# Up products on the unscaled residual, scaled in PSUM, with every second residual addition on GpSimd

## The chip, the cores and the metric

The kernel runs on one core of a Trainium2 chip. Five engines work side by side, each with its own in-order instruction queue: TensorE (PE, matmuls into PSUM), VectorE (DVE), ScalarE (ACT), GpSimd (POOL, which doesn't reach PSUM) and SyncE (SP, which here issues DMAs). They wait for each other on semaphores. The metric is the device time of one execution in microseconds, and lower is better.

## The reference, cut to what matters

The program computes a first block of two layers (attention and a recurrent mixer side by side, then a feed-forward part and an embedding gate) and a second block of two layers, on 512 tokens of width 1024, all in float32. The change touches one place of the first block's layers:

```python
x = x + rmsnorm(mixed @ w_out, norm_mix_post)
h = rmsnorm(x, norm_ffn_pre)                      # y * rsqrt(mean(y*y) + eps) * gain
u = causal_dwconv(h @ w_up, conv_w, conv_b)       # three taps along the tokens, per channel
ua, ub = _split(u, (FFN_DIM, FFN_DIM))            # 2816 = 22 tiles of 128 each
x = x + rmsnorm((jax.nn.gelu(ua) * ub) @ w_down, norm_ffn_post)
```

The root-mean-square factor of a token multiplies its whole row of `h`, so it can be taken out of the product `h @ w_up`: scaling each token's column of the product gives the same numbers.

## The kernel before, in words

Activations lie transposed: 128 partitions of channels, then tiles of 128 channels (KD = 8 for the width), then 512 tokens. The residual is `xT` [128, 8, 512]. A matmul makes a tile of 128 output channels by 512 tokens, one PSUM bank; there are 8 banks, of which bank 6 holds the spread factor of a norm (`rstd`) or the running sums of the modulation, and bank 7 the column sums of a norm.

For accuracy each float32 operand is split into a high part (rounded to the fast matmul format) and a low part (the rest). A product is three matmuls per k tile (`split_matmuls`, L232): high x high weight, low x high weight, high x low weight, so 24 for a tile over the width. Weights come as a stream of units of 512 KB in the order of use. For each unit SP loads it into one of two raw buffers (L309), ACT copies it to its high part `Whi` (L284), GpSimd subtracts to get the low part `Wlo` (`low_parts`, L299), into one of three slots. `HighParts.upto` lets ACT make a high part only once the unit three before is used up; ACT, GpSimd and SP do this at fixed places of their queues. SP loads a unit once the low part of the unit two before is done, and issues the modulation weights (`ada_load`) between the units of the feed-forward part.

At the change the order is this. The out projection leaves `yT`. Its norm "n2" is made: squares on ACT, sums over channels on PE (`column_sums`, 16 records of one column each, L178), root on ACT (L146), reciprocal on DVE (L217), spread of the four token columns to a [128, 512] factor on PE (`norm_spread_pe`, L205). Then `residual_dve` (L1854, L1857) does eight times a multiplication T (`yT` by gain and factor into `t2`) and an addition A (`xT` + `t2`). ACT squares each new tile (L133), PE sums it, and after the eighth comes the root, the reciprocal and the spread of norm "n3". Only then `split_dve` and `split_act` make the scaled tile (L392), its high part `hh` on ACT (L367) and its low part `hl` on DVE (L386), tile by tile, and PE starts the first two up products together (`split_pair`: for each k tile three matmuls for the one and three for the other, as soon as `hl` is there).

The feed-forward part follows a list, `FFN1`: up products (i, 0) and (i, 1) for i = 0 to 21, into banks 2(i % 2) and 2(i % 2) + 1, with the down products of eight hidden tiles put in after i = 9 and 17 and at the end. For each up product ACT makes `acc` = bank x tap 2 + bias (L1992), DVE adds taps 1 and 0 (L2043, L2046); ACT's gelu (L1974) of (i, 0) goes back into its bank, DVE multiplies with (i, 1) (L2023), ACT makes the high part `gh` (L1980) and DVE the low part `gl` (`g_low`, L2027). PE may start (i, 0) once `g_low(i - 2)` is done. During the first 48 entries of the list DVE also does two modulation steps each (`mods_dve`, L336, L340). PE's sums for these steps are L349.

Of the kernel before, what the change touches and what calls it, by code (L numbers as in the profile page):

```python
# [18 lines left out]
F32 = mybir.dt.float32  # L19
# [8 lines left out]
P = 128  # L28
# [1774 lines left out]
    mixed_low_dve(dve, s, b, KD - 2, KD)  # L1803


def split_product(pe, ps, w, b):

    for k in range(KD):
        last = split_matmuls(pe, ps, columns_of(w, 1, at=k * P), tiles_of(b["hh"][:, k:k + 1], b["hl"][:, k:k + 1]), 1,
                             start=k == 0, stop=k == KD - 1)  # L1810
    return last


def split_pair(pe, ready, banks, units, b, done):

    for k in range(KD):
        pe.wait_ge(ready, k + 1)
        for ps, w in zip(banks, units):
            last = split_matmuls(pe, ps, columns_of(w, 1, at=k * P), tiles_of(b["hh"][:, k:k + 1], b["hl"][:, k:k + 1]), 1,
                                 start=k == 0, stop=k == KD - 1)  # L1820
            if k == KD - 1:
                last.then_inc(done, 1)


def project_pe(pe, s, b, ring, done, copied, ready, name, later=None):
# [15 lines left out]
def copy_act(act, b, mm, copied, dst, high, first, after, n=8, func=ACT.Copy):  # L1841
    for m in range(n):
        high.around(act, first + m)
        act.wait_ge(mm, m + 1)
        act.activation(dst[:, m], b["ps"][:, m % 4], func).then_inc(copied, 1)
        after(m)


def residual_dve(dve, s, b, step, y, gain):
# [75 lines left out]
def ffn_pe(pe, s, b, ring):  # L1925
    for at, key in enumerate(FFN1[0]):
        if 0 <= at - SUM_LAG < MODS and (at - SUM_LAG) % ADA_N == ADA_N - 1:
            mods_pe(pe, s, b, (at - SUM_LAG) // ADA_N)
        if key[0] == "up":
            i, j = key[1:]  # L1930
            if i == 0:
                if j == 0:
                    pair = [ring.take(pe) for _ in range(2)]
                    split_pair(pe, s["h2_lo"], [b["ps"][:, x] for x in range(2)], pair, b, s["up_p"])
                continue
            w = ring.take(pe)
            if i >= 2:
                pe.wait_ge(*((s["up_v"], UP_V(i - 2, "b2")) if j else (s["g_lo"], i - 1)))
            split_product(pe, b["ps"][:, 2 * (i % 2) + j], w, b).then_inc(s["up_p"], 1)
        elif key[1] < PARTS1 - 1:  # L1940
            down_pe(pe, s, b, ring, key[1], key[2], FT)
        elif key[2] >= OPEN:
            down_pe(pe, s, b, ring, key[1], key[2], FT)
            if key[2] == KD - 1:
                summed_squares_pe(pe, s, b, "n4")
        elif key[2] == 0:
            pe.wait_ge(s["mods_v"], 1)
            last_down_pe(pe, s, b, ring, FT)
# [22 lines left out]
def ffn_act(act, s, b, high, first):  # L1971
    def gelu(i):
        act.wait_ge(s["up_v"], UP_V(i, "a2"))
        act.activation(b["ps"][:, 2 * (i % 2)], b["acc"][:, 2 * (i % 2)], ACT.Gelu_apprx_tanh).then_inc(s["up_ge"], 1)  # L1974

    def g_high(i):
        act.wait_ge(s["up_g"], i + 1)
        if i >= GRING:
            act.wait_ge(s["dn_p"], KD * ((i - GRING) // PART + 1))
        act.activation(b["gh"][:, i % GRING], b["ps"][:, 2 * (i % 2)], ACT.Copy).then_inc(s["g_hi"], 1)  # L1980

    for key in FFN1[0]:
        high.around(act, first + FFN1[1][key])
        if key[0] == "up":
            i, j = key[1:]
            slot = 2 * (i % 2) + j
            if j == 1:
                gelu(i)
            act.wait_ge(s["up_p"], 2 * i + j + 1)
            if i >= 2 and j == 1:  # L1990
                act.wait_ge(s["up_g"], i - 1)
            act.activation(b["acc"][:, slot], b["ps"][:, slot], ACT.Identity, scale=b["p"]("cw2", j * FT + i),  # L1992
                           bias=b["p"]("cb", j * FT + i)).then_inc(s["up_a"], 1)
            if j == 0 and i:
                g_high(i - 1)
            if j == 1 and i == FT - 1:
                high.upto(act, first + FFN1[1][("down", PARTS1 - 1, OPEN - 1)] + 1)
                table_act(act, b, "n4", ACT.Sqrt)
                g_high(i)
        elif key[1] == PARTS1 - 1:  # L2000
            for m in (key[2] - 1,) if key[2] < KD - 1 else range(key[2] - 1, KD):
                if m >= 0:
                    act.wait_ge(s["dn_v"], KD * (PARTS1 - 1) + m + 1)
                    summed_square_act(act, s, b, "n4", m, b["yT"][:, m])
# [13 lines left out]
def ffn_dve(dve, s, b):  # L2018
    def product(i):
        dve.wait_ge(s["up_ge"], i + 1)  # L2020
        dve.wait_ge(s["up_v"], UP_V(i, "b2"))
        bank = b["ps"][:, 2 * (i % 2)]
        dve.tensor_tensor(bank, bank, b["acc"][:, 2 * (i % 2) + 1], MUL).then_inc(s["up_g"], 1)  # L2023

    def g_low(i):
        dve.wait_ge(s["g_hi"], i + 1)
        dve.tensor_tensor(b["gl"][:, i % GRING], b["ps"][:, 2 * (i % 2)], b["gh"][:, i % GRING].bitcast(F32), SUB).then_inc(s["g_lo"], 1)  # L2027

    for at, key in enumerate(FFN1[0]):
        if at == MODS + SUM_LAG + 1:  # L2030
            dve.wait_ge(s["m_p"], MODS)
            dve.tensor_copy(b["mods"][:, b["layer"]], b["ps"][:, b["norm_bank"], 0:MODS]).then_inc(s["mods_v"], 1)
        if key[0] == "down":
            down_dve(dve, s, b, key[1], key[2])
            if key[1] == PARTS1 - 1:
                square_sum_dve(dve, s, b, "n4", key[2] - 2)
            if at < MODS:
                mods_dve(dve, s, b, at)
            continue
        i, j = key[1:]  # L2040
        slot = 2 * (i % 2) + j
        dve.wait_ge(s["up_a"], UP_A(i, ("ca", "cb")[j]))
        dve.scalar_tensor_tensor(out=b["acc"][:, slot, 1:TOK], in0=b["ps"][:, slot, 0:TOK - 1], scalar=b["p"]("cw1", j * FT + i),  # L2043
                                 in1=b["acc"][:, slot, 1:TOK], op0=MUL, op1=ADD).then_inc(s["up_v"], 1)
        dve.wait_ge(s["up_v"], UP_V(i, "ab"[j] + "1"))
        dve.scalar_tensor_tensor(out=b["acc"][:, slot, 2:TOK], in0=b["ps"][:, slot, 0:TOK - 2], scalar=b["p"]("cw0", j * FT + i),  # L2046
                                 in1=b["acc"][:, slot, 2:TOK], op0=MUL, op1=ADD).then_inc(s["up_v"], 1)
        if j == 0 and i:
            g_low(i - 1)
        if j == 1:  # L2050
            product(i)
            if i == FT - 1:
                g_low(i)
        if at < MODS:
            mods_dve(dve, s, b, at)

# [39 lines left out]
def first_block(nc, b, stream, stream_after, ple, ada, positions):  # L2098
# [1 line left out]
        [f"ada_in{i}" for i in range(ADA)] + ["md_v", "m_p", "mods_v"] + [f"w_in{i}" for i in range(RAW)] + ["w_hi", "w_lo", "ple_in", "zeroed", "x_out", "x_back"] + \  # L2100
        norms("n2", "n3", "n4", "n5", "nx") + [n + x for n in ("h1", "h2") for x in SPLIT_SEMS] + \
        ["res1", "res2", "res3"] + RWKV_SEMS + ATT_SEMS + ["gate_p", "gate_a", "gate_v", "mx_hi", "mx_lo", "wo_p", "wo_z"] + \
        ["up_p", "up_a", "up_v", "up_ge", "up_g", "g_hi", "g_lo", "dn_p", "dn_v", "p_hi", "p_lo", "e_p", "e_z",
         "h3_hi", "h3_lo", "pg_p", "pg_z", "pg_v"]
    with ExitStack() as ctx:
        s, every = semaphores(ctx, nc, names)
# [10 lines left out]
        with ExitStack() as c:  # L2117
# [17 lines left out]
            with ExitStack() as c2:  # L2135
                sb(c2, "yT", KD, TOK)
                with ExitStack() as c3:
                    for name in ("gh", "gl"):
                        sb(c3, name, GRING, TOK, dt=F32R)
                    for name, *shape in (("acc", 4, TOK), ("ada", ADA, UNIT), ("macc", 2, ADA_W)):  # L2140
                        sb(c3, name, *shape)
                with ExitStack() as c3:
                    sb(c3, "pT", 2, TOK)
# [7 lines left out]
        for layer in range(LAYERS):  # L2151
            enter_layer(b, layer, stream[layer], stream[layer + 1] if layer + 1 < LAYERS else stream_after[0])
            with nc.Block() as block:
# [32 lines left out]
                def _(pool):  # L2186
# [7 lines left out]
                    attention_masks(pool, s, b)  # L2194
                    low_parts(pool, s, b, AT_ATT + 8, AT_GATE + 3)
                    attention_pool(pool, s, b)
                    low_parts(pool, s, b, AT_GATE + 3, AT_E + 2)
                    pool.wait_ge(s["p_hi"], 1)
                    pool.tensor_tensor(b["pl"][:], b["pT"][:], b["ph"][:].bitcast(F32), SUB).then_inc(s["p_lo"], 1)
                    low_parts(pool, s, b, AT_PG, AT_PG + 1)  # L2200
# [8 lines left out]
                def _(pe):  # L2209
# [8 lines left out]
                    pe.wait_ge(s["gate_a"], 16)  # L2218
                    project_pe(pe, s, b, ring, s["wo_p"], s["wo_z"], s["mx_lo"], "n2")
                    norm_spread_pe(pe, s, b, "n2")  # L2220
                    norm_pe(pe, s, b, "n3", KD)
                    ffn_pe(pe, s, b, ring)
                    norm_spread_pe(pe, s, b, "n4")
                    for m in range(KD):
# [15 lines left out]
                def _(act):  # L2240
# [19 lines left out]
                    def square_y(m):  # L2260
                        act.wait_ge(s["wo_z"], m + 1)
                        summed_square_act(act, s, b, "n2", m, b["yT"][:, m])
                    copy_act(act, b, s["wo_p"], s["wo_z"], b["yT"], high, AT_WO, square_y)
                    norm_root_act(act, s, b, "n2", 1, D)
                    norm_act(act, s, b, "n3", lambda i: b["xT"][:, i], KD, D, lambda i: (s["res1"], 2 * i + 2))
                    split_act(act, s, "h2", b, b["hh"], KD)
                    ffn_act(act, s, b, high, AT_FFN)
                    norm_root_act(act, s, b, "n4", 1, D)
                    act.wait_ge(s["ple_in"], 16)
# [21 lines left out]
                def _(dve):  # L2291
# [8 lines left out]
                        square_sum_dve(dve, s, b, "n2", i)  # L2300
                    norm_dve(dve, s, "n2", b)
                    dve.wait_ge(s["x_back"], 16)
                    residual_dve(dve, s, b, s["res1"], b["yT"], lambda i: b["p"]("mix_post", i))
                    norm_dve(dve, s, "n3", b)
                    split_dve(dve, s, "h2", b, scaled(dve, b, b["xT"], lambda i: b["p"]("ffn_pre", i)), b["hh"], b["hl"], KD)
                    dve.wait_ge(s["tab_out"], 32)
                    ffn_dve(dve, s, b)
                    norm_dve(dve, s, "n4", b)
# [862 lines left out]
```

## Time and profile before

| | us |
|---|---|
| median of 3 runs | 3939.98 (3936.72 to 3941.65) |
| span of the profiled execution (first to last instruction) | 3931.4 |
| own time of the profiled execution | not listed apart from its span |
| PE busy | 3743.9 (95%) |
| DVE busy | 1848.1 (47%) |
| ACT busy | 1581.7 (40%) |
| POOL busy | 1779.5 (45%) |
| DMA | 379.88 MB, mean 97 GB/s |
| mean granted TensorE clock | 0.979 |

Busy time counts the instructions on the engine itself, not its waits. A timeline row gives the start in us from the span's start, the duration, the engine, the line of the kernel, what it writes and reads, and in brackets how long the engine idled before it and what ended that. The granted clock is 1.00 at 2.4 GHz and 0.50 at 1.2 GHz.

### The profile page before, as it was taken

The page shows a single profiled execution, that of the slowest core. Times are in us where ns is not written, and L with a number is a line of the kernel's source. Part 1 is how long each engine was busy: PE and PEld are TensorE (multiplying, and loading weights), DVE is VectorE, ACT ScalarE, POOL GpSimd, SP SyncE. Part 2 cuts the span into 40 slices and gives each one's busy share as a digit, 9 for nine tenths or more (in the row PEclk, how much of TensorE's full clock was granted, in tenths as well). Part 3 has the DMA queues.
Part 4 walks back from the last instruction along what each step waited for, and adds up shares of the span by engine and source line. Part 5 has one row for each costly group of instructions (what it writes and reads, how often), then busy time and mean ns, then how long its engine had stood idle before and what let it go on. Part 6 is the DMA issues. An engine that isn't in the chain of part 4 may idle for free. (4 is left out here: it accounts for less than half of the span.)

```text
span 3931.4 us, 72626 instructions
## 1 busy us (share of the span) xinstructions
PE 3743.9 (95%) x30890; PEld 3040.7 (77%) x30904; DVE 1848.1 (47%) x2868; ACT 1581.7 (40%) x2643; POOL 1779.5 (45%) x1132
## 2 busy tenths in 40 slices
PE   7999989999998999998999999899999999999998
PEld 6777758878887777776887887677878877787887
DVE  7777652155635877754226553543231133423112
ACT  5555352343334555535234333454332234433222
POOL 5555444434445555544443444463444435344443
PEclk9999999989998999999998999899999999999999
DMA  4111203335532211122334553212222221222322
GB/s 142 52 56 56 88 28 135 99 134 193 183 107 76 92 51 56 56 99 72 99 105 143 189 182 104 69 65 76 97 86 97 97 85 66 70 96 87 97 97 86
DMA packets 108753, 379.88 MB, mean 97 GB/s; under 512 B 12560, under 2 KB 12944, under 8 KB 107792
## 3 DMA queue, kind: packets, MB, share of 16 engines
q1 hardware_dynamic: 102816, 365.66, 27.8%
q10 hardware_dynamic: 5616, 9.58, 0.7%
q8 instruction: 246, 4.03, 0.4%
q14 instruction: 75, 0.61, 0.1%
HBM read 359.46 MB, written 15.73 MB: 95 GB/s over the span
## 5 line engine op out<-in xcount | busy, mean ns | idle before, releaser
L299 POOL TENSOR_TENSOR Wlo<-raw,Whi 128x1024 fp32r<-128x1024 f32 (+1 forms) x744 | 1385.8, 1876 | 1671.6 <-ACT Whi L284 1671.4
L232 PE MATMUL ps<-hh,Whi 128*128 128x512 f32 x2864 | 1150.9, 402 | 22.1 <-DVE hl L383 10.1
L232 PE MATMUL ps<-hl,Whi 128*128 128x512 f32 x2864 | 1125.3, 393 | 0.0
L232 PE MATMUL ps<-hh,Wlo 128*128 128x512 f32 x2864 | 1124.4, 393 | 0.1
L284 ACT ACTIVATE Whi<-raw 128x1024 fp32r<-128x1024 f32 x552 | 578.7, 1054 | 689.3 <-PE ps L232 617.8
L232 PEld LDWEIGHTS ps<-hh,Whi 128*128 128x128 f32 x2864 | 543.3, 190 | 147.8 <-issue 15.7
L232 PEld LDWEIGHTS ps<-hh,Wlo 128*128 128x128 f32 x2864 | 543.0, 190 | 116.2 <-issue 0.5
L232 PEld LDWEIGHTS ps<-hl,Whi 128*128 128x128 f32 x2864 | 543.8, 190 | 108.1 <-issue 1.9
L232 PE MATMUL ps<-gh,Whi 128*128 128x512 f32 x864 | 337.9, 391 | 3.8 <-POOL Wlo L299 3.8
L232 PE MATMUL ps<-gh,Wlo 128*128 128x512 f32 x864 | 336.5, 390 | 0.0
L232 PE MATMUL ps<-gl,Whi 128*128 128x512 f32 x864 | 336.5, 389 | 0.0
L1146 POOL TENSOR_TENSOR TM<-TD,const 128x256 f32<-128x256 f32 x192 | 157.4, 843 | 152.3 <-PE ps L719 75.7
L1799 DVE TENSOR_TENSOR sg<-sg,ps 128x512 f32<-128x512 f32 x64 | 44.0, 688 | 366.9 <-PE ps L232 366.6
L232 PEld LDWEIGHTS ps<-gh,Whi 128*128 128x128 f32 x864 | 162.2, 188 | 39.0 <-POOL Wlo L299 5.5
L232 PEld LDWEIGHTS ps<-gh,Wlo 128*128 128x128 f32 x864 | 162.2, 188 | 33.8
L232 PEld LDWEIGHTS ps<-gl,Whi 128*128 128x128 f32 x864 | 162.3, 188 | 33.2
L2736 DVE SCALAR_TENSOR_TENSOR xT<-ps,mod,xT 128x512 f32<-128x512 f32 x64 | 48.1, 752 | 281.7 <-PE ps L232 281.7
L1992 ACT ACTIVATE acc<-ps,par 128x512 f32<-128x512 f32 x88 | 68.6, 780 | 273.5 <-PE ps L232 273.5
L2726 DVE TENSOR_TENSOR gt<-gt 128x512 f32<-128x512 f32 x64 | 47.9, 749 | 256.8 <-ACT gt L2614 256.8
L2043 DVE SCALAR_TENSOR_TENSOR acc<-ps,par,acc 128x511 f32<-128x511 f32 x88 | 66.0, 750 | 197.7 <-ACT acc L1992 197.7
L1782 ACT ACTIVATE sg<-ps 128x512 f32<-128x512 f32 x64 | 38.3, 599 | 239.2 <-PE ps L232 239.2
L719 PEld LDWEIGHTS ps<-X,TM 64*64 64x64 f32 x2560 | 81.8, 135 | 55.7 <-DVE y L1216 32.1
(365 smaller groups left out, 5652.8 us busy)
## 6 DMA issues: line engine op xcount, KB each, us to landing
raw<-in_stream SPq DMA_DIRECT2D x554, 512.0 KB, 3.3
ada<-in_ada SPq DMA_DIRECT2D x96, 512.0 KB, 4.3
park_x<-xT SPq DMA_DIRECT2D x2, 2048.0 KB, 7.3
park_yh<-yh ACTq DMA_DIRECT2D x16, 256.0 KB, 2.1
park_yl<-yl ACTq DMA_DIRECT2D x16, 256.0 KB, 2.5
xT<-park_x SPq DMA_DIRECT2D x2, 2048.0 KB, 8.3
yrh<-park_yh SPq DMA_DIRECT2D x16, 256.0 KB, 5.1
yrl<-park_yl SPq DMA_DIRECT2D x16, 256.0 KB, 4.9
```

The lines of the kernel that those rows point to most:

```text
L232: last = pe.matmul(ps, left[a](k), right[c](k), start=start and k == 0 and i == 0, stop=stop and k == n - 1 and i == 2)
L284: act.activation(self.b["Whi"][:, weight_slot(self.b, u)], self.b["raw"][:, raw_slot(self.b, u)], ACT.Copy).then_inc(self.s["w_hi"], 1)
L299: last = pool.tensor_tensor(b["Wlo"][:, slot, part], b["raw"][:, raw_slot(b, u), part], b["Whi"][:, slot, part].bitcast(F32), SUB)
L719: return pe.matmul(b["ps"][half(u), bank, block(c)], left[:, block(c)], right[:, block(c)], start=True, stop=True)
L1146: pool.tensor_tensor(blocks(b["TM"][:, h, l % 2]), blocks(b["TD"][:, h]), lvl[:, l].broadcast_to([P, BLK, CB]), MUL) .then_inc(s["inv_g"], 1)
L1782: act.activation(b["sg"][:, i], b["ps"][:, i], ACT.Sigmoid).then_inc(s["gate_a"], 1)
L1799: dve.tensor_tensor(b["sg"][:, i], b["sg"][:, i], b["ps"][:, 4 + i], MUL).then_inc(s["gate_v"], 1)
L1992: act.activation(b["acc"][:, slot], b["ps"][:, slot], ACT.Identity, scale=b["p"]("cw2", j * FT + i), bias=b["p"]("cb", j * FT + i)).then_i ...
L2043: dve.scalar_tensor_tensor(out=b["acc"][:, slot, 1:TOK], in0=b["ps"][:, slot, 0:TOK - 1], scalar=b["p"]("cw1", j * FT + i), in1=b["acc"][: ...
L2726: dve.tensor_tensor(b["gt"][:, i % 4], b["gt"][:, i % 4], b["gt"][:, i % 4], MUL).then_inc(s["f1_v"], 1)
L2736: dve.scalar_tensor_tensor(out=b["xT"][:, m], in0=b["ps"][:, 4 + i % 3], scalar=b["mod"][:, 40 + m:41 + m], in1=b["xT"][:, m], op0=MUL, op ...
```

## The change: what it does

`hh` and `hl` are now made from `xT` times the gain alone, without the factor of norm "n3": ACT's high part is a copy with a scale, DVE's low part is one multiply-and-subtract (`raw_low`). They can follow each addition at once. `shared_residual_dve` does all eight T, the additions of tiles 0, 2, 4 and 6, and the low part of the tile before; `shared_residual_pool` does the additions of tiles 1, 3, 5 and 7 on GpSimd. ACT copies and squares each tile. `summed_pair` on PE does the first two up products tile by tile and puts the column sum of norm "n3" behind each tile's six matmuls. The spread of "n3" moves into product (1, 0), behind its first k tile; ACT stores the spread factor as `r3`. Every one of the 44 up products is then multiplied with `r3` in its bank by DVE (semaphore `up_n`) before ACT reads it. On DVE, `g_low` of the tile before and the modulation steps move ahead of the two tap additions; on ACT, `g_high` moves ahead of `acc`. ACT makes the high part of the third up unit ahead of the root of "n2", and GpSimd its low part ahead of its additions.

```diff
-def split_product(pe, ps, w, b):
+def split_product(pe, ps, w, b, amid=None):
     for k in range(KD):
+        if amid and k == amid[0]:
+            amid[1]()
...
+def summed_pair(pe, s, b, name, banks, units, done):
+    for k in range(KD):
+        pe.wait_ge(s["h2_lo"], k + 1)
+        for ps, w in zip(banks, units):
+            last = split_matmuls(pe, ps, columns_of(w, 1, at=k * P), tiles_of(b["hh"][:, k:k + 1], b["hl"][:, k:k + 1]), 1,
+                                 start=k == 0, stop=k == KD - 1)
+            if k == KD - 1:
+                last.then_inc(done, 1)
+        norm_sum_pe(pe, s, b, name, k, KD)
...
+def raw_low(dve, s, b, i, gain):
+    dve.wait_ge(s["h2_hi"], i + 1)
+    dve.scalar_tensor_tensor(out=b["hl"][:, i], in0=b["xT"][:, i], scalar=gain, in1=b["hh"][:, i].bitcast(F32), op0=MUL, op1=SUB) \
+        .then_inc(s["h2_lo"], 1)
+
+def added(s, i):
+    return s["add_g" if i % 2 else "add_v"], i // 2 + 1
+
+def shared_residual_dve(dve, s, b, gain, pre):
+    for i in range(KD):
+        if i >= 2:
+            dve.wait_ge(*added(s, i - 2))
+        dve.scalar_tensor_tensor(out=b["t2"][:, i % 2], in0=b["yT"][:, i], scalar=gain(i), in1=b["rstd"][:], op0=MUL, op1=MUL) \
+            .then_inc(s["res1"], 1)
+        if i % 2 == 0:
+            dve.wait_ge(s["res1"], i + 1)
+            dve.tensor_tensor(b["xT"][:, i], b["xT"][:, i], b["t2"][:, i % 2], ADD).then_inc(s["add_v"], 1)
+        for k in (i - 1,) if i < KD - 1 else (i - 1, i):
+            if k >= 0:
+                raw_low(dve, s, b, k, pre(k))
+
+def shared_residual_pool(pool, s, b):
+    for i in range(1, KD, 2):
+        pool.wait_ge(s["res1"], i + 1)
+        pool.tensor_tensor(b["xT"][:, i], b["xT"][:, i], b["t2"][:, i % 2], ADD).then_inc(s["add_g"], 1)
...
@@ ffn_pe @@
-                    split_pair(pe, s["h2_lo"], [b["ps"][:, x] for x in range(2)], pair, b, s["up_p"])
+                    summed_pair(pe, s, b, "n3", [b["ps"][:, x] for x in range(2)], pair, s["up_p"])
...
-            split_product(pe, b["ps"][:, 2 * (i % 2) + j], w, b).then_inc(s["up_p"], 1)
+            split_product(pe, b["ps"][:, 2 * (i % 2) + j], w, b, amid=(1, lambda: norm_spread_pe(pe, s, b, "n3")) if i == 1 and j == 0 else None) \
+                .then_inc(s["up_p"], 1)
@@ ffn_act @@
             if j == 1:
                 gelu(i)
-            act.wait_ge(s["up_p"], 2 * i + j + 1)
+            elif i:
+                g_high(i - 1)
+            act.wait_ge(s["up_n"], 2 * i + j + 1)
...
-            if j == 0 and i:
-                g_high(i - 1)
@@ ffn_dve @@
+        if i == 0 and j == 0:
+            dve.wait_ge(s["r3_a"], 1)
+        dve.wait_ge(s["up_p"], 2 * i + j + 1)
+        dve.tensor_tensor(b["ps"][:, slot], b["ps"][:, slot], b["r3"][:], MUL).then_inc(s["up_n"], 1)
+        if j == 0 and i:
+            g_low(i - 1)
+        if at < MODS:
+            mods_dve(dve, s, b, at)
         dve.wait_ge(s["up_a"], UP_A(i, ("ca", "cb")[j]))
...
-        if j == 0 and i:
-            g_low(i - 1)
...
-        if at < MODS:
-            mods_dve(dve, s, b, at)
@@ first_block: GpSimd, PE, ACT, DVE @@
-                    low_parts(pool, s, b, AT_GATE + 3, AT_E + 2)
+                    low_parts(pool, s, b, AT_GATE + 3, AT_FFN + SLOTS)
+                    pool.wait_ge(s["x_back"], 16)
+                    shared_residual_pool(pool, s, b)
+                    low_parts(pool, s, b, AT_FFN + SLOTS, AT_E + 2)
...
-                    norm_pe(pe, s, b, "n3", KD)
...
+                    high.upto(act, AT_FFN + SLOTS)
                     norm_root_act(act, s, b, "n2", 1, D)
-                    norm_act(act, s, b, "n3", lambda i: b["xT"][:, i], KD, D, lambda i: (s["res1"], 2 * i + 2))
-                    split_act(act, s, "h2", b, b["hh"], KD)
+                    for i in range(KD):
+                        act.wait_ge(*added(s, i))
+                        act.activation(b["hh"][:, i], b["xT"][:, i], ACT.Copy, scale=b["p"]("ffn_pre", i)).then_inc(s["h2_hi"], 1)
+                        norm_square_act(act, s, b, "n3", i, b["xT"][:, i])
+                    norm_root_act(act, s, b, "n3", KD, D)
+                    act.wait_ge(s["n3_sp"], 1)
+                    act.activation(b["r3"][:], b["rstd"][:], ACT.Copy).then_inc(s["r3_a"], 1)
...
-                    residual_dve(dve, s, b, s["res1"], b["yT"], lambda i: b["p"]("mix_post", i))
-                    norm_dve(dve, s, "n3", b)
-                    split_dve(dve, s, "h2", b, scaled(dve, b, b["xT"], lambda i: b["p"]("ffn_pre", i)), b["hh"], b["hl"], KD)
+                    shared_residual_dve(dve, s, b, lambda i: b["p"]("mix_post", i), lambda i: b["p"]("ffn_pre", i))
+                    dve.wait_ge(s["n3_rt"], 1)
+                    dve.reciprocal(b["rt"][:], b["rt"][:]).then_inc(s["n3_rs"], 1)
```

## Rows read from the trace of the kernel before

**Rows 1.** Page, part 1: busy us (share of span) xinstructions, by engine.

```profile
PE 3743.9 (95%) x30890; PEld 3040.7 (77%) x30904; DVE 1848.1 (47%) x2868; ACT 1581.7 (40%) x2643; POOL 1779.5 (45%) x1132
```

**Rows 2.** Windows: length, busy us by engine, PEclk, DMA share, GB/s.

```profile
802.10:822.40 20.30, 11.66 (x186) 10.19 (x185) 13.48 (x22) 8.05 (x14) 0.00 (x0) 0.59 0.18 52
835.10:1160.00 324.90, 324.90 (x1585) 266.89 (x1584) 170.63 (x241) 115.51 (x146) 141.67 (x59) 1.00 0.49 172
2059.10:2079.80 20.70, 12.09 (x185) 10.44 (x185) 13.43 (x22) 8.05 (x14) 0.00 (x0) 0.56 0.17 53
```

**Rows 3.** Timeline, DVE: start, us, engine, line, operation, tiles [idle before].

```profile
804.47 0.18 DVE L217 RECIPROCAL rt<-rt 128x4 f32<-128x4 f32 x1 [11.18 <-ACT rt L146]
805.39 0.75 DVE L1854 SCALAR_TENSOR_TENSOR t<-yT,par,ps 128x512 f32<-128x512 f32 x1 [0.74 <-PE ps L205]
806.18 0.69 DVE L1857 TENSOR_TENSOR xT<-xT,t 128x512 f32<-128x512 f32 x1
...
2062.85 0.75 DVE L1854 SCALAR_TENSOR_TENSOR t<-yT,par,ps 128x512 f32<-128x512 f32 x1 [1.21 <-PE ps L205]
```

**Rows 4.** Timeline of ACT, same columns.

```profile
804.18 0.26 ACT L146 ACTIVATE rt<-ps,const 128x4 f32<-128x4 f32 x1 [0.73 <-PE ps L178]
806.90 0.63 ACT L133 ACTIVATE sq<-xT 128x512 f32<-128x512 f32 x1 [2.46 <-DVE xT L1857]
...
830.51 1.04 ACT L284 ACTIVATE Whi<-raw 128x1024 fp32r<-128x1024 f32 x1
...
840.76 0.78 ACT L1992 ACTIVATE acc<-ps,par 128x512 f32<-128x512 f32 x1 [0.84 <-PE ps L232]
...
846.20 0.78 ACT L1992 ACTIVATE acc<-ps,par 128x512 f32<-128x512 f32 x1 [1.34 <-PE ps L232]
...
2104.63 0.78 ACT L1992 ACTIVATE acc<-ps,par 128x512 f32<-128x512 f32 x1 [1.33 <-PE ps L232]
```

**Rows 5.** Timeline of PE at the hole of the first layer.

```profile
804.71 0.65 PE L205 MATMUL ps<-const,rt 128*128 128x128 f32 x4 [0.58 <-DVE rt L217]
807.59 1.02 PE L178 MATMUL ps<-const,sq 128*64 128x1 f32 x16 [2.23 <-ACT sq L133]
...
822.38 0.77 PE L232 MATMUL ps<-hh,Whi 128*128 128x512 f32 x1 [2.39 <-DVE hl L386]
...
824.22 0.63 PE L232 MATMUL ps<-hl,Whi 128*128 128x512 f32 x1
824.65 0.63 PE L232 MATMUL ps<-hh,Wlo 128*128 128x512 f32 x1
```

**Rows 6.** Timeline of PE around one column sum between two products, second block.

```profile
3263.14 0.39 PE L232 MATMUL ps<-hh,Wlo 128*128 128x512 f32 x1
3263.46 0.63 PE L178 MATMUL ps<-const,sq 128*64 128x1 f32 x16
3264.02 0.50 PE L232 MATMUL ps<-hh,Whi 128*128 128x512 f32 x1
```

**Rows 7.** Timelines, GpSimd and DVE; line L2205 (ns min/median/max).

```profile
831.64 2.39 POOL L299 TENSOR_TENSOR Wlo<-raw,Whi 128x1024 fp32r<-128x1024 f32 x1 [30.22 <-ACT Whi L284]
...
1199.31 2.50 DVE L1857 TENSOR_TENSOR xT<-xT,t 128x512 f32<-128x512 f32 x1
...
L2205 POOL TENSOR_TENSOR hl<-xT,hh x16: 1280/1567/1752, 1205.5 to 2478.1; 128x512 fp32r<-128x512 f32 x16
```

**Rows 8.** Windows of PE: busy us (instructions), then PEclk, the granted clock.

```profile
806.00:818.00 12.00, 7.87 (x126) 0.50 0.03 12
822.40:826.10 3.70, 3.70 (x9) 0.50 0.02 4
2079.80:2085.60 5.80, 5.78 (x14) 0.50 0.01 1
```

**Rows 9.** DVE in the products: timeline row of L2023, and a window's busy time.

```profile
840.65 0.70 DVE L2023 TENSOR_TENSOR ps<-ps,acc 128x512 f32<-128x512 f32 x1
...
860.00:900.00 40.00, 25.40 (x37) 1.00 0.53 188
```

More of the change, by code:

```diff
@@ L2102, in first_block @@
         ["res1", "res2", "res3"] + RWKV_SEMS + ATT_SEMS + ["gate_p", "gate_a", "gate_v", "mx_hi", "mx_lo", "wo_p", "wo_z"] + \
-        ["up_p", "up_a", "up_v", "up_ge", "up_g", "g_hi", "g_lo", "dn_p", "dn_v", "p_hi", "p_lo", "e_p", "e_z",
+        ["add_v", "add_g", "up_p", "up_n", "r3_a", "up_a", "up_v", "up_ge", "up_g", "g_hi", "g_lo", "dn_p", "dn_v", "p_hi", "p_lo", "e_p", "e_z",
          "h3_hi", "h3_lo", "pg_p", "pg_z", "pg_v"]
@@ L2139, in first_block @@
                         sb(c3, name, GRING, TOK, dt=F32R)
-                    for name, *shape in (("acc", 4, TOK), ("ada", ADA, UNIT), ("macc", 2, ADA_W)):
+                    for name, *shape in (("r3", TOK), ("acc", 4, TOK), ("ada", ADA, UNIT), ("macc", 2, ADA_W)):
                         sb(c3, name, *shape)
```

## The prediction

> **What bounds the kernel now.** I read the page first: TensorE (PE) is busy 95% of the span, DVE 47%, ACT 40% [rows 1]. So time can be won only where PE waits. The windows of the stages show where that is around the change. In the up and down products (835.1 to 1160.0) PE is busy 324.90 of 324.90 us at the granted clock 1.00, which is 2.4 GHz. Just ahead of them, 802.1 to 822.4, it is busy 11.66 of 20.30 us, at 0.59 on average; the second layer has the same hole, 12.09 of 20.70 us [rows 2]. The change works in these two holes and in the 44 up products behind each. The timelines of DVE, ACT and PE then give the chain in the hole: residual multiplication (T, L1854) and addition (A, L1857) on DVE, eight times; squares on ACT; column sums on PE; root; spread; only then the scaled and split tiles and, at 822.38, the first up matmul [rows 3 to 5]. I measure each layer from the first T (805.39 and 2062.85) to ACT's reading of the fourth up product, called (1,1), at 846.20 and 2104.63 [rows 3, 4]: 40.81 and 41.78 us. From there on PE is the bound, and what is won up to it is won at the end.
>
> The profiled execution has a span of 3931.4 us; the runs' median is 3939.98, 8.6 us more, which lies around the span. I work out differences in the span and add them to the median.
>
> **The change, part by part.** *Ahead of the chain.* ACT now makes the high part of the third up unit (1.04 us) before the root, where it idled 0.73 us [rows 4]: +0.3 us. GpSimd's low part of that unit (2.39 us [rows 7]) moves forward too and runs from about 804.5 to 806.9; SP then issues its next weight load and modulation load some 25 us earlier, into a DMA that is busy 0.18 here [rows 2], at no cost. The first A, at 806.5, reads two SBUF operands. Such an A took 2.50 us beside a low part, against 0.69 alone [rows 7, 3]. It would wait here until 806.9: +0.45 (bounds 0 and 1.8).
>
> *First matmul.* T to A 0.79, the wait 0.45, A 0.69, ACT's scaled copy 0.63 (the square's row [rows 4]), the new low part L 0.75 (as T), hand-overs 0.35: 3.65 us after T. With the 0.3 PE starts at 809.35, where it was 822.38. If GpSimd's first addition gets the port ahead of L, add up to 1.3.
>
> *GpSimd's additions.* Their nearest row is its 128x512 subtraction, 1.28 to 1.75 us [rows 7]. For two tiles DVE has two T, one A and two L, about 3.4 us; when the two-operand ones wait for GpSimd, 3.9 to 4.4. The last L is then ready between 823.5 and 825.3, while PE, by the next part, reaches the last tile at 823.5 at the earliest: PE's pace covers them. Without that cover (PE at full clock throughout, 1.75 for each addition) they would cost 1.8 us a layer. The Trainium skill (GPSIMD Engine Reference, Engine selection) advises elementwise work on VectorE, because two-input operations take about twice as long on GpSimd. By that rule alone four additions, each some 0.7 us longer, would add 2.8 us a layer; the rows agree on the ratio, but the chain they would lengthen is not PE's.
>
> *The pair with the sums in it.* Each of eight k tiles is six matmuls and one column sum of 16 records. At 2.4 GHz a product of 24 matmuls takes 5.44 us (846.20 less 840.76 [rows 4]), 0.227 each, and a sum between products takes 0.88 - 0.23 = 0.65 [rows 6]: 1.36 + 0.65 = 2.01 per tile, 16.1 in all. At 1.2 GHz they start 0.43 apart and a sum takes 1.02 [rows 5]; with 0.1 for the switch 2.56 + 1.12 = 3.7, 29.6 in all. So it matters how long PE stays at 1.2 GHz after 809.35. If that is x us, the pair lasts 16.1 + 0.457x (0.457 = 1 - 2.01/3.7).
>
> *What x is.* No row shows this mixture; both of its parts have rows. Sums alone (busy 7.87 of 12 us) leave the clock at 0.50, and matmuls back to back have it at 0.50 for 3.7 us in one layer and 5.8 in the other before it rises [rows 8]. The bounds are therefore 4.8 (the mean of these) and 29.6 (the whole pair). Weighted by the mixture, 70% matmuls, it would be 12.2; the middle of the bounds is 17.2. The mixture is nearer to back-to-back matmuls, but not the same, so I take 14.5, between the two.
>
> *Behind the pair.* Product (1,0) is 5.44 us, and the spread in its middle 0.65 [rows 5]: PE would be done with it 6.1 us after the pair. The root chain up to the spread hides under three matmuls (0.26 and 0.18 [rows 4, 3] against 0.68). What is late next is the unit of (1,1): its high part stands on ACT behind the first acc, which waits for the new multiplication, which waits for the stored spread. Root 0.26, reciprocal 0.18, spread 0.65, copy 0.63 (as the square), multiplication 0.70 (a row with PSUM in and out [rows 9]), acc 0.78, high part 1.04, low part 2.39, hand-overs 0.5: 7.1. So PE waits 1.0 us there, and (1,1) is read 7.1 + 5.44 + 0.05 = 12.6 after the pair.
>
> *The sum.* 809.35 + 16.1 + 0.457x + 12.6 = 838.05 + 0.457x against 846.20: -8.15 + 0.457x. The second layer was 0.97 us longer before and starts alike: -9.1 + 0.457x. With x = 14.5: -1.5 and -2.5, together **-4.0 us: 3936**.
>
> *In the products.* The 88 added multiplications (0.70 each, 62 us of DVE) I cost at nothing: PE hides them. DVE is busy 25.40 of 40 us early in the products [rows 9], 3.45 per 5.44 us of a product; 4.15 with the new one. The longest new chain, product to multiplication to acc to two convolution steps to product to low part, has a whole further product's time on PE in front of its consumer. Queued behind the waiting multiplication on DVE are only g_low and the modulation steps. With that cover gone the price is rival 3's.
>
> **The rivals.**
> 1. *The clock comes back as promptly as behind dense products*: x = 4.8 in both layers, -6.0 and -6.9, **3927**. For it: matmuls are 70% of the mixture, and once the clock is up, products with sums between them keep it there [rows 6]. Against: in neither layer did a rise come with sums running.
> 2. *The clock stays at 1.2 GHz through the pair* (the slower side). Then x = 29.6, and product (1,0) begins at half speed as well: 2.4 us lost there, of which the 1.0 us wait covers part, so 1.4. -8.15 + 13.5 + 1.4 = +6.8, and +5.8: **3952.6**. It decides from x = 18 on, where the gain is gone. For it: the sums of the kernel before hold 0.50 although PE is busy two thirds of the time [rows 8], and the change puts one behind every sixth matmul. Against: full-width matmuls still take most of each tile. The Trainium skill (TensorE: Matmul & The Clock Gate, "A second HAM failure mode") tells of a kernel whose short idle times between groups of matmuls kept dropping its clock; by that the time would be this rival's, and no row here shows such a mixture at 1.2 GHz.
> 3. *DVE becomes the bound of the products*: all 88 multiplications come to stand on PE's path, +62 us, **4002**. It decides when DVE's work per product passes 5.44 us; 4.15 speaks against it, and a mixture of waits at the start of the products is all that speaks for it.
>
> That the change doesn't do what it says (first matmul not earlier, because A or L waits) would need more than 12 us of port waits; the rows give 3 at most.
>
> **How the numbers follow.** Forecast (x between about 8 and 22, so 3930 to 3943) 0.43; rival 1 0.30; rival 2 0.21; rival 3 0.04; the rest 0.02. A measurement of this kernel can tell about 0.2%, 7.9 us, from no change. Faster by more: rival 1 and the forecast's fast end, 0.35. Slower by more: rivals 2 and 3, 0.25. Within: 0.40. The range runs from a little below rival 1 to rival 2, 3926 to 3952; DVE-bound and worse is left out.
>
> **What would show it.** In the profile after: the first up matmul some 13 us earlier than before after the first T; a low part of 2.4 us under the first A; PE without idle through the pair; the granted clock 0.50 there for x us, which by itself puts the result between rivals 1 and 2; a wait of PE of about 1 us for the low part ahead of (1,1); no idle of PE from there to the down products. Wrong would be PE waiting for L inside the pair (then the additions or the port set the pace), PE waiting for g_low in the products, or a time outside 3926 to 3952.

## The result and the profile after

The changed kernel takes 3944.45 us (median of 20 runs, 3934.87 to 3952.25) against 3939.1 us for the kernel before (3932.5 to 3944.16, 20 runs): ratio 1.0015, interval 1.0008 to 1.0022. It is slower by 5.3 us, inside the range and inside the 0.2%, but not in the direction of the forecast, and the interval leaves out 1. The spread of its runs has grown as well, from 11.7 to 17.4 us. The profiled execution has a span of 3942.2 us.

PE, busy for 3743.9 us before [rows 1], is now busy for longer, although no product was added (page, part 1):

```profile
PE 3759.3 (95%) x30904; PEld 3045.7 (77%) x30904; DVE 1894.1 (48%) x2932; ACT 1589.8 (40%) x2645; POOL 1790.9 (45%) x1140
```

The windows at the two holes of [rows 2] say why. Columns: stretch and length, busy us of PE, PEld, DVE, ACT and POOL with instructions, granted clock, DMA share, GB/s. Of each layer the first row runs up to the first up matmul.

```profile
802.10:813.79 11.69, 6.03 (x70) 4.75 (x68) 4.63 (x6) 4.76 (x9) 6.00 (x3) 0.83 0.50 169
813.79:816.60 2.81, 2.81 (x6) 1.78 (x6) 2.77 (x5) 1.31 (x3) 0.18 (x1) 0.50 0.24 96
816.60:832.24 15.64, 15.64 (x171) 11.71 (x170) 10.29 (x12) 6.99 (x11) 4.10 (x3) 1.00 0.01 2
832.24:839.35 7.11, 6.19 (x32) 4.82 (x29) 5.05 (x9) 5.08 (x7) 2.38 (x1) 1.00 0.00 0
839.35:1160.00 320.65, 320.65 (x1564) 263.30 (x1565) 193.03 (x278) 114.12 (x142) 139.34 (x58) 1.00 0.48 171
2059.10:2069.97 10.87, 5.21 (x66) 4.07 (x64) 4.62 (x6) 4.24 (x8) 5.79 (x3) 0.81 0.52 171
2069.97:2100.00 30.03, 30.03 (x171) 21.63 (x172) 11.26 (x16) 8.18 (x14) 4.25 (x3) 0.50 0.02 10
2100.00:2110.90 10.90, 9.98 (x53) 7.98 (x52) 8.40 (x13) 6.74 (x10) 4.79 (x2) 1.00 0.23 85
```

The same instructions run in both layers. In the first the clock is back at 2.4 GHz 2.8 us after the first up matmul; in the second PE works through nearly the whole pair, 30.0 us without idle, at 1.2 GHz. The timeline of PE in the second layer (start, us, engine, line, operation, tiles, idle before) shows two tiles there: 3.78 us from 2069.97 to 2073.75 and 3.80 from there to 2077.55. Six matmuls 0.43 apart make 2.6 of that; the column sum and the switches to and from it make the other 1.2. The rows before to compare are [rows 5].

```profile
2069.97 0.77 PE L232 MATMUL ps<-hh,Whi 128*128 128x512 f32 x1 [4.66 <-DVE hl L1866]
...
2072.24 0.63 PE L232 MATMUL ps<-hh,Wlo 128*128 128x512 f32 x1
2072.80 1.02 PE L178 MATMUL ps<-const,sq 128*64 128x1 f32 x16
2073.75 0.79 PE L232 MATMUL ps<-hh,Whi 128*128 128x512 f32 x1
...
2077.55 0.79 PE L232 MATMUL ps<-hh,Whi 128*128 128x512 f32 x1
```

As the measure of a layer I take the time from its first T to its first down matmul, since PE has no idle from the fourth product to there. The rows of the down matmul (before, then after) and of the second layer's first T after:

```profile
936.21 0.39 PE L232 MATMUL ps<-gh,Whi 128*128 128x512 f32 x1
2194.64 0.39 PE L232 MATMUL ps<-gh,Whi 128*128 128x512 f32 x1
...
935.18 0.39 PE L232 MATMUL ps<-gh,Whi 128*128 128x512 f32 x1
2203.16 0.39 PE L232 MATMUL ps<-gh,Whi 128*128 128x512 f32 x1
...
2065.35 0.75 DVE L1879 SCALAR_TENSOR_TENSOR t<-yT,par,ps 128x512 f32<-128x512 f32 x1 [0.74 <-PE ps L205]
```

With the first T of [rows 3] and the one at 809.16 below this makes 130.82 and 131.79 us before, 126.01 and 137.81 after: 4.8 gained, 6.0 lost.

The remaining 9.6 of the 10.8 us between the two profiled spans lie outside these stretches. Of them 3.8 are there before the first T (805.39 before, 809.16 after), where the change moves only one weight unit's high part (+0.3 in the prediction), and 3.5 lie between the first layer's down matmul and the second layer's first T, which took 1126.6 us before and 1130.2 after. Both vary from profile to profile: in two further profiles of the changed kernel the second took 1130.1 and 1126.8.

The timelines of DVE and GpSimd at the start of the first layer, to compare with [rows 3] and [rows 7]:

```profile
809.16 0.75 DVE L1879 SCALAR_TENSOR_TENSOR t<-yT,par,ps 128x512 f32<-128x512 f32 x1 [0.74 <-PE ps L205]
809.95 1.08 DVE L1883 TENSOR_TENSOR xT<-xT,t 128x512 f32<-128x512 f32 x1
810.95 0.73 DVE L1879 SCALAR_TENSOR_TENSOR t<-yT,par,ps 128x512 f32<-128x512 f32 x1
811.82 1.82 DVE L1866 SCALAR_TENSOR_TENSOR hl<-xT,par,hh 128x512 fp32r<-128x512 f32 x1
```

```profile
808.13 2.34 POOL L299 TENSOR_TENSOR Wlo<-raw,Whi 128x1024 fp32r<-128x1024 f32 x1 [3.03 <-ACT Whi L284]
811.83 1.26 POOL L1893 TENSOR_TENSOR xT<-xT,t 128x512 f32<-128x512 f32 x1 [1.35 <-DVE t L1879]
```

The first addition took 1.08 us beside the low part of the weights, and the first low part 1.82 beside GpSimd's first addition. PE's two waits in the first layer are the one ahead of the pair and the one foreseen ahead of product (1,1):

```profile
813.79 0.76 PE L232 MATMUL ps<-hh,Whi 128*128 128x512 f32 x1 [4.66 <-DVE hl L1866]
...
839.35 0.50 PE L232 MATMUL ps<-hh,Whi 128*128 128x512 f32 x1 [0.92 <-POOL Wlo L299]
```

### The profile page after: what moved, and what is told of

Its sections match the earlier page's. It is cut to its first block and busy times, and to the rows that moved or that the text cites. A ratio compares the mean times of both kernels' runs of the same rounds, so it can differ in the third digit from the quotient of the medians.

```text
span 3942.2 us, 72688 instructions
## 1 busy us (share of the span) xinstructions
PE 3759.3 (95%) x30904; PEld 3045.7 (77%) x30904; DVE 1894.1 (48%) x2932; ACT 1589.8 (40%) x2645; POOL 1790.9 (45%) x1140
## 3 DMA queue, kind: packets, MB, share of 16 engines
q8 instruction: 246, 4.03, 0.4%
## 5 line engine op out<-in xcount | busy, mean ns | idle before, releaser
L2674 ACT ACTIVATE gt<-ps 128x512 f32<-128x512 f32 x64 | 38.4, 601 | 213.4 <-PE ps L232 213.4
```

The costliest lines, as they stand in the source:

```text
L2674: act.activation(b["gt"][:, i % 4], b["ps"][:, i % 4], ACT.Relu).then_inc(s["f1_a"], 1)
```

## The experiments

**Three at the cause.** Theory A: how soon the clock comes back differs from layer to layer, as if drawn; the column sums between the matmuls can keep it at 1.2 GHz. Theory B: the loss lies outside the holes. Theory C: GpSimd's additions pace the pair.

*The changed kernel again.* No edit.

> The changed kernel once more, unchanged. Theory A (the clock decides, layer by layer: either PE is back at 2.4 GHz about 3 us after the first up matmul and the layer gains some 5 us, or the column sum behind every sixth matmul keeps it at 1.2 GHz through the pair of 30 us and the layer loses some 6 us): in each layer one of these two pictures, nothing between, not necessarily the same ones as in the first profile; time 3926 to 3953. Theory B (the loss lies outside the holes, since the profile after is also some 6 us later in stretches that the change does not touch): the same stretches are late again by the same amounts, whatever the pair does. Theory C (GpSimd's additions pace the pair): PE waits for low parts inside the pair.

Measured: 3954.66 us. The windows from the first up matmul to the rise of the clock:

```profile
818.16:844.30 26.14, 26.14 (x148) 18.79 (x148) 11.26 (x16) 8.15 (x14) 4.25 (x3) 0.50 0.03 11
844.30:847.50 3.20, 3.20 (x37) 2.48 (x36) 0.18 (x1) 0.26 (x1) 0.00 (x0) 1.00 0.00 0
2084.34:2110.70 26.36, 26.36 (x152) 19.02 (x153) 11.27 (x16) 8.15 (x14) 4.25 (x3) 0.50 0.03 12
```

Both layers lost (136.10 and 136.22 us to the first down matmul, 5.3 and 4.4 more than before). The rise came behind the matmuls of the pair's seventh tile of eight, so "nothing between" was too strict, and the time is 2 us above the bound given. The first T is 4.4 us later than in the first profile with the same program: what lies outside the holes varies by itself. PE has no idle in the pair, which is against theory C.

*Matmuls without use ahead of the pair.*

```diff
+def filler(pe, bank, unit, n):
+    for _ in range(n):
+        pe.matmul(bank, unit[0][:, 0:P], unit[0][:, 0:TOK], start=True, stop=True)
...
                     pair = [ring.take(pe) for _ in range(2)]
+                    filler(pe, b["ps"][:, 0], pair[0], 11)
                     summed_pair(pe, s, b, "n3", ...)
```

> 11 full-width matmuls without use (weights by weights, into the bank that the pair then starts anew) between the spread of n2 and the first up matmul, where PE idled 4.65 us: 11 x 0.43 = 4.7 us at 1.2 GHz, 2.5 at 2.4. Theory A: PE is dense before the sums begin, the clock is back by the first or second tile of the pair in both layers, the pair lasts 17 to 20 us in both, each layer gains about 5 us on the kernel before: about 3929, some 15 us below the changed kernel. Theory B: stays at 3944 give or take 3. Theory C: stays near 3944, PE waits for low parts.

Measured: 3927.12 us, ratio 0.9973 (0.9963 to 0.9982). PE in the first layer:

```profile
811.87 0.65 PE L205 MATMUL ps<-const,rt 128*128 128x128 f32 x4 [0.68 <-DVE rt L217]
812.27 4.35 PE L1830 MATMUL ps<-Whi 128*128 128x512 f32 x11
817.13 0.50 PE L232 MATMUL ps<-hh,Whi 128*128 128x512 f32 x1 [0.50 <-DVE hl L1872]
...
818.72 0.63 PE L178 MATMUL ps<-const,sq 128*64 128x1 f32 x16
819.28 0.49 PE L232 MATMUL ps<-hh,Whi 128*128 128x512 f32 x1
```

And the windows of the filler and of the pair:

```profile
812.27:816.00 3.73, 3.73 (x13) 2.95 (x12) 3.28 (x4) 1.24 (x2) 2.38 (x2) 0.55 0.51 186
816.00:835.20 19.20, 18.70 (x183) 13.61 (x182) 12.80 (x18) 9.09 (x15) 5.71 (x4) 1.00 0.10 40
...
2069.54:2087.60 18.06, 18.06 (x180) 13.41 (x181) 11.67 (x17) 8.52 (x15) 5.20 (x3) 1.00 0.04 15
```

The fillers ran mostly at 1.2 GHz, the clock rose under them, and the pair with all its sums ran at 2.4 GHz in both layers: 124.69 and 124.70 us to the first down matmul, 6.1 and 7.1 less than before. More work on PE, and the kernel is 17 us faster than the changed one. In these layers the mixture keeps the clock up once it is up; it does not reliably raise it. Theories B and C had 3944.

*Column sums of one matmul instead of eight.*

```diff
-        norm_sum_pe(pe, s, b, name, k, KD)
+        pe.wait_ge(s[name + "_sq"], k + 1)
+        pe.matmul(b["ps"][half(0), b["norm_bank"], 0:1], b["sq"][:, k % 2, 0:64], b["c"]("ones")[:, 0:1],
+                  start=k == 0, stop=k == KD - 1, skip_group_check=True).then_inc(s[name + "_ss"], 1)
```

> Each column sum inside the pair is cut to one record of its eight (the sum is incomplete: the scaling is not the right one, every wait stays). Theory A: without the sums PE is nearly dense from the first up matmul at 1.2 GHz, the granted clock is back at 1.00 within 6 us in both layers, then the pair runs at the pace of the low parts (about 2.2 us a tile): 17 to 20 us, a gain of 4 to 7 us in each layer: about 3928. Theory B: 3944 less at most 4. Theory C: PE waits for low parts in every tile and the time stays near 3944.

This kernel leaves out seven eighths of each sum, so its scaling is wrong and it serves for the time alone. Measured: 3926.58 us, ratio 0.9974 (0.9963 to 0.9984). The clock was back 5.4 and 5.6 us after the first up matmul, as behind dense matmuls before [rows 8]:

```profile
810.29:815.70 5.41, 5.40 (x13) 3.95 (x14) 5.10 (x8) 2.67 (x5) 1.72 (x1) 0.50 0.14 56
815.70:827.77 12.07, 12.07 (x55) 8.24 (x54) 6.56 (x10) 5.88 (x10) 3.02 (x2) 1.00 0.00 0
2066.18:2071.80 5.62, 5.62 (x14) 3.92 (x14) 5.31 (x8) 2.66 (x5) 1.73 (x1) 0.50 0.13 55
2071.80:2083.80 12.00, 12.00 (x56) 8.29 (x55) 6.24 (x10) 5.88 (x10) 3.03 (x2) 1.00 0.00 0
```

So it is the sums that keep the clock down. The layers take 124.19 and 124.30 us to the first down matmul, 0.5 and 0.4 less than with filler and whole sums. That is a balance of two terms: at 2.4 GHz a tile takes 1.79 us here (816.24 to 818.04) against 2.15 with the whole sum, 2.9 us less in eight tiles, and the 5.4 us at 1.2 GHz take some 2.3 back (a tile there takes 3.13). PE did not wait for a low part either, so the pace of 2.2 us a tile that was expected from the low parts did not show.

**Four at GpSimd's share.** *All additions on DVE.*

```diff
 def added(s, i):
-    return s["add_g" if i % 2 else "add_v"], i // 2 + 1
+    return s["add_v"], i + 1
...
-        if i % 2 == 0:
+        if True:
             dve.wait_ge(s["res1"], i + 1)
...
-                    pool.wait_ge(s["x_back"], 16)
-                    shared_residual_pool(pool, s, b)
```

> GpSimd's four additions go back to DVE, all else as in the changed kernel. Theory A: the first up matmul comes about 1.1 us earlier (the first low part took 1.82 us beside GpSimd's addition instead of 0.75), the clock in the pair is drawn anew in each layer: -2 us against the changed kernel on average, 3942, with the same spread of 3930 to 3952. Theory B: 3942 to 3944. Theory C: 10 us faster, the pair 16 us in both layers.

Measured: 3938.67 us (3925.64 to 3951.46, 12 runs), ratio 0.9995 (0.9983 to 1.0006). The first up matmul comes 3.66 us after the first T instead of 4.62. DVE:

```profile
807.19 0.75 DVE L1879 SCALAR_TENSOR_TENSOR t<-yT,par,ps 128x512 f32<-128x512 f32 x1 [1.21 <-PE ps L205]
807.97 0.69 DVE L1883 TENSOR_TENSOR xT<-xT,t 128x512 f32<-128x512 f32 x1
...
809.96 0.74 DVE L1866 SCALAR_TENSOR_TENSOR hl<-xT,par,hh 128x512 fp32r<-128x512 f32 x1
```

The clock rose in the middle of the pair here:

```profile
810.85:829.60 18.75, 18.75 (x108) 13.50 (x110) 12.20 (x18) 6.16 (x10) 0.00 (x0) 0.50 0.06 23
...
2069.99:2092.50 22.51, 22.51 (x130) 16.21 (x130) 12.94 (x19) 7.40 (x12) 0.00 (x0) 0.50 0.05 22
```

The gain on the changed kernel, 5.8 us between the medians, is three times what was expected; 1 us a layer is the first low part, and theory C's 10 us did not come. The next three runs were meant to find the rest of it.

*Only the addition of tile 1 back on DVE.*

```diff
 def added(s, i):
-    return s["add_g" if i % 2 else "add_v"], i // 2 + 1
+    return (s["add_g"], i // 2) if i % 2 and i > 1 else (s["add_v"], i + 1 if i < 2 else i // 2 + 2)
...
-        if i % 2 == 0:
+        if i % 2 == 0 or i == 1:
...
-    for i in range(1, KD, 2):
+    for i in range(3, KD, 2):
```

> DVE makes the addition of tile 1 too, GpSimd keeps those of tiles 3, 5 and 7. The question is how the 5.8 us between the changed kernel (3944.5) and the one with all additions on DVE (3938.7) come about. Theory D (only the first low part's wait beside GpSimd's first addition costs, 0.96 us a layer directly and the rest through when the pair starts): the first up matmul 3.7 us after the first T, the time as with all on DVE, 3939. Theory E (each addition on GpSimd costs in the pair): 3942 or more. The clock in the pair is drawn anew in each layer, so the median moves by some us either way.

Measured: 3939.14 us (3925.26 to 3948.07, 12 runs), ratio 1.0010 (1.0001 to 1.0018) to a kernel before that ran at 3935.35 in this series. By the time it is theory D, by the ratio it lies between; the two theories are not told apart. The first up matmul came 4.06 us after the first T, not 3.7: the first addition took 1.08 us beside the weights' low part. The profiled execution was the fastest of the twelve (3925.26 us), and in it the clock was back 3.1 and 3.2 us after the first up matmul.

*Two more profiles*, without an edit, of the changed kernel and of the one with all additions on DVE.

> The changed kernel a third time, for two more layers: how long PE stays at 1.2 GHz after the first up matmul. So far 2.8, 30.0, 26.1 and 26.4 us. If the duration is drawn anew each time, it need not agree with those; the layer's gain should follow it at 0.46 us per us.

> All additions on DVE a second time, for two more layers. So far PE stayed at 1.2 GHz for 18.8 and 22.5 us of the pair. If undoing GpSimd's share shortens it by itself, both new layers are again below the changed kernel's 26 to 30; if it is a draw, anything from 3 to 30.

Measured: 3943.43 and 3931.52 us. The changed kernel stayed at 1.2 GHz for 29.9 us of the pair in one layer and 15.1 in the other; with all additions on DVE it was 2.8 and 3.0, after 18.8 and 22.5 in the profile before. So short and long stretches come with either. All six layers of the changed kernel, sorted by x, the time at 1.2 GHz after the first up matmul:

| x, us | 2.8 | 15.1 | 26.1 | 26.4 | 29.9 | 30.0 |
|---|---|---|---|---|---|---|
| first T to first down matmul, us | 126.01 | 130.90 | 136.10 | 136.22 | 137.72 | 137.81 |
| fall of the clock to 1.2 GHz, us ahead of the first up matmul | 3.99 | 5.44 | 4.56 | 4.39 | 4.20 | 4.06 |

The layer follows x at (137.81 - 126.01)/(30.0 - 2.8) = 0.434 us per us. The mean of the six is 134.13, 2.8 above the 131.30 of the kernel before: 5.6 us in two layers, where the medians differ by 5.3.

The table's last row shows what goes with x. The stretches from the fall of the clock to the first up matmul are, in the two layers of the first profile after, in the first layer of the second profile with all additions on DVE, and in the second layer of the changed kernel's last profile (just ahead of each the clock is at 1.00):

```profile
809.80:813.79 3.99, 0.00 (x1) 0.04 (x1) 3.82 (x5) 1.91 (x4) 1.94 (x2) 0.50 0.61 202
2065.91:2069.97 4.06, 0.00 (x1) 0.03 (x1) 3.89 (x5) 1.91 (x4) 2.02 (x2) 0.50 0.67 234
...
810.91:814.94 4.03, 0.00 (x1) 0.03 (x1) 3.96 (x6) 2.02 (x4) 1.29 (x1) 0.50 0.50 185
...
2072.18:2077.62 5.44, 1.11 (x5) 0.75 (x5) 4.07 (x6) 1.90 (x4) 3.33 (x2) 0.50 0.64 229
```

Twelve layers have whole sums and no filler: six of the changed kernel, four with all additions on DVE, two with tile 1 on DVE. In the five with x of 2.8 to 3.2 the clock had fallen 3.59 to 4.03 us ahead of the first up matmul; in the other seven it had fallen 4.06 to 5.44 us ahead, and the earlier it fell, the shorter is x, from 30.0 down to 15.1. This order was seen afterwards; no run moved the fall by itself, so that it decides is not shown.

**Three for a better version.** *Filler and all additions on DVE* (both edits above).

> The eleven matmuls without use, and all eight additions on DVE. With the clock held, what GpSimd's share itself costs is seen apart from the clock. Theory A: only the first low part's wait goes (first up matmul 3.66 us after the first T as with all additions on DVE, instead of 4.57), from then on PE's own pace of 2.16 us a tile rules, DVE's 2.2 us a tile is level with it: 0.9 us a layer, 3925 where the filler alone had 3927. If a rise of the clock comes later because the filler has a shorter gap to run in, the gain is nil. Theory C (GpSimd's additions pace the pair): the pair falls from 18 to 16 us or less, 3921. The other way round (the additions do relieve DVE): DVE at 2.2 us or more a tile sets the pace, 3929.

Measured: 3923.38 us, ratio 0.9967 (0.9955 to 0.9979); 124.08 and 124.12 us to the first down matmul. With the clock held, GpSimd's share costs 0.6 us a layer in the traces. The first up matmul came at 3.99 us, not 3.66, again with an addition of 1.11 us beside the weights' low part.

*The same, and the fourth unit's high part ahead of the root.*

```diff
+                    high.upto(act, AT_FFN + SLOTS + 1)
                     norm_root_act(act, s, b, "n3", KD, D)
                     act.wait_ge(s["n3_sp"], 1)
```

> As the run with filler and all additions on DVE, and ACT makes the high part of the fourth unit ahead of the root of n3 instead of behind the first convolution tap, so that its low part is there when PE wants it. If PE's wait of 0.92 us ahead of the fourth product is the chain root, reciprocal, spread, scaling, tap, high part, low part, as predicted, the wait goes and each layer gains 0.9 us: 3923. If the high part delays the root (it may start when the first product of the pair is through, 1.3 us before the last column sum is, and takes 1.05), some of that comes back, at most 0.5. Rival: PE waits for the scaling itself: no change.

Measured: 3918.53 us, ratio 0.9959 (0.9947 to 0.9972), the fastest here. ACT's timeline:

```profile
827.46 1.06 ACT L284 ACTIVATE Whi<-raw 128x1024 fp32r<-128x1024 f32 x1 [2.47 <-PE ps L232]
828.66 0.27 ACT L146 ACTIVATE rt<-ps,const 128x4 f32<-128x4 f32 x1 [0.15 <-PE ps L178]
829.99 0.60 ACT L2332 ACTIVATE r<-ps 128x512 f32<-128x512 f32 x1 [1.06 <-PE ps L205]
```

The root still waits for the last sum (0.15), so the high part was free; PE's wait ahead of (1,1) is gone, and the layers take 122.72 and 123.04 us, 1.4 and 1.1 less than without this edit. The medians differ by 4.9 us, more than these two; the intervals of the two ratios overlap.

*The kernel before, with fillers.*

```diff
+    filler(pe, b["ps"][:, 0], pair[0], 5)
+    for i in range(KD):
+        norm_sum_pe(pe, s, b, "n3", i, KD)
+        if i < KD - 1:
+            filler(pe, b["ps"][:, 0], pair[0], 1)
+    norm_spread_pe(pe, s, b, "n3")
+    filler(pe, b["ps"][:, 0], pair[0], 5)
```

> The kernel before with matmuls without use in its own hole: five behind the spread of n2, one behind each column sum of n3, five behind the spread of n3. What of the gain of the filler is had without the change: the clock is back by the first up matmul, which saves about half of the 3.7 and 5.8 us that the up products ran at 1.2 GHz, 2 to 3 us a layer; one filler and one sum at 1.2 GHz take 1.45 us, the pace of the residual, so little is lost ahead of it: 3934. Theory A puts the change with the filler well below this (3927 was measured); if it comes to 3927 here too, the early products earned nothing.

Measured: 3939.77 us, ratio 1.0011 (1.0002 to 1.0020): slower, where 3934 was expected.

```profile
809.60 2.02 PE L1928 MATMUL ps<-Whi 128*128 128x512 f32 x5
812.08 1.02 PE L178 MATMUL ps<-const,sq 128*64 128x1 f32 x16 [0.46 <-ACT sq L133]
813.02 0.79 PE L1928 MATMUL ps<-Whi 128*128 128x512 f32 x1
813.75 1.02 PE L178 MATMUL ps<-const,sq 128*64 128x1 f32 x16
814.70 0.79 PE L1928 MATMUL ps<-Whi 128*128 128x512 f32 x1
```

A sum and one filler take 1.67 us (812.08 to 813.75), not 1.45, which is more than the residual's pace, so the hole grew from 17.0 to 18.9 us. One matmul behind each sum leaves the clock at 0.50, as in the kernel before; with the five fillers ahead of them the up products then ran at 1.2 GHz for 1.8 and 2.1 us instead of 3.7 and 5.8, which the longer hole outweighs (131.94 and 132.01 us to the first down matmul). This is not the best filler for that kernel; it shows only that useless matmuls are no gain in themselves.

## Why the prediction was wrong

**The step that failed is x**, the time at 1.2 GHz after the first up matmul, put at 14.5 us. The prediction bounded it nearly rightly (4.8 to 29.6; 2.8 to 30.0 was seen) and priced it nearly rightly (0.457 per us; 0.434). It failed where it chose: "The mixture is nearer to back-to-back matmuls, but not the same, so I take 14.5". At 1.2 GHz the mixture is nearer to the sums alone: in four of six layers PE stayed at half clock for 26 to 30 us, and the mean is 21.7. The prediction's own break-even was 18: with 21.7 in place of 14.5 its sum turns from -4.0 to +2.6 us, so this step alone turns the sign. Rival 2 was the likelier picture of a single layer, at a chance of 0.21, and I took both layers to go the same way, though the same program gave 2.8 and 30.0 within one execution; the time of one execution can then be anything between the two rivals. Why x differs is open; what goes with it is how long ahead of the first up matmul the clock had fallen, a term that the prediction does not have.

**Smaller terms of the sum.** The first up matmul was put 3.65 us after the first T and came at 4.62: the first low part L took 1.82 us beside GpSimd's first addition and 0.74 with all additions on DVE. This is the "up to 1.3" that the sum left out. A tile at 2.4 GHz was put at 2.01 us and takes 2.15 (817.13 to 819.28 in the filler run), 1.1 more in eight; the first matmul behind a sum takes 0.49 instead of 0.39, which [rows 6] shows already (0.50). These two, 2.1 us a layer, are the difference between the -6.9 that the sum gives for x = 2.8 and the measured -4.8, and they move the break-even down to some 14. With the +2.6 above, 4.2 in two layers make +6.8, a little over the 5.6 of the table. With x = 30.0 the second layer lost 6.0, where rival 2 had 5.8; that it is so near is luck. Rival 2 counts 1.4 for product (1,0) at half speed, but the clock was back at 2100.0 and (1,0) ran at 2.4 GHz; the late first matmul (1.0) and a pair of 30.3 us instead of 29.6 stand in its place.

**What held.** DVE's 88 multiplications are hidden: from 839.35 to 1160 PE is busy 320.65 of 320.65 us, in the second layer 322.63 of 322.63 from 2107.37 to 2430, and rival 3 is out. PE's wait ahead of (1,1) was 0.92 us (1.0 predicted), its chain the one named, since moving one link took it away. PE does not wait for a low part inside the pair. The move of the up products itself was worth having: with the clock held it gains 6.1 and 7.1 us. That this is also rival 1's gain (6.0 and 6.9) is luck: rival 1 has 4.8 us at 1.2 GHz, the filler runs none, and the smaller terms that rival 1 lacks make up for it. Some 1.9 and 2.9 of the gain (half of 3.7 and 5.8, an estimate) are the half-speed stretch of the kernel before, which the filler takes away too, so the move itself is worth some 4.2 a layer.

The Trainium skill (TensorE: Matmul & The Clock Gate, "A second HAM failure mode") tells of an engine that idles for moments between groups of matmuls and so keeps changing its clock; the rows agree on the loss but not on the cause, as PE was busy 30.03 of 30.03 us at 0.50, with column sums where that page has idle time. The advice of the Trainium skill (GPSIMD Engine Reference, Engine selection) to keep elementwise work on VectorE fits the 0.6 to 1 us a layer that GpSimd's share cost directly, not the 2.8 that were worked out from it.

**What stays open.** Why the fall of the clock and x go together, and whether GpSimd's additions also make a long x likelier: the changed kernel's ratio is 1.0015 (1.0008 to 1.0022), that with all additions on DVE 0.9995 (0.9983 to 1.0006), and the run between, at 1.0010, does not tell. By the order in the table they would: the first up matmul comes 4.62 us after the first T in five of the changed kernel's six layers and 4.06 in the last profile with all additions on DVE, and 0.56 us less would put five of the six falls at 4.0 us ahead or nearer. That is an estimate which no run tests, and in the other profile with all additions on DVE, where the clock fell 5.19 and 4.80 us ahead, both x were long.

## What to carry to other kernels

When small matmuls are moved in between large ones, ask first at which clock PE will enter the mixture: a busy PE is not a PE at full clock, and a mixture that holds 2.4 GHz need not reach it. If PE stands idle ahead of such a stretch, a few full-width matmuls without use there can be worth more than the work that was moved; here they turned +5 us into -11. And a term whose two bounds decide the sign is better forecast as two cases, judged stage by stage, than by a value between them.

## What the runs showed of the hardware that was not expected

The same instructions in the same order ran at 0.50 for 2.8 us in one layer and 30.0 in the other, with PE without idle in both; the clock had fallen 3.99 us ahead of the first up matmul in the one and 4.06 in the other. Column sums cut to one of their eight matmuls let the clock rise within 5.6 us; whole ones mostly did not. And the work ahead of the first T, nearly the same in all these kernels, ended anywhere from 805.39 to 813.54 us; in the records of the granted clock short drops stand at differing places there (before: at 338, 519 and 526 us; after: at 144, 243, 390, 523 and 530).
